# Stick-breaking attention: weights taken as differences of the running product, with value rows differenced instead

## What is computed

```
mask = s_idx < t_idx
log1m = jnp.where(mask, -jax.nn.softplus(z), 0.0)
after = lax.cumsum(log1m, axis=3, reverse=True) - log1m
logw = jax.nn.log_sigmoid(z) + after
w = jnp.where(mask, jnp.exp(...logw...), 0.0)
out = jnp.einsum('bhqk,bhkd->bhqd', w, vb)
```

## Time and profile before

| | |
|---|---|
| median of 3 runs | 2482.05 us (2480.07 to 2483.8) |
| the profiled execution | 2482.8 us, of which the trace spans 2480.7 us |
| PE busy | 2379.0 us, 96% of the span |
| DVE, ACT, POOL busy | 1497.8, 962.1, 672.5 us |
| the values (from the evict of block 0) | 1375 to 1418 us of the span |
| the attention stage | 1418 to 1695 us of the span |

### The profile page before, as it was taken

How to read it: one execution, slowest core, us unless ns; L and a number is a source line. 1 busy time by engine, 2 the same in 40 slices (tenths; PEclk the granted TensorE clock), 3 DMA queues, 4 the chain that set the end, 5 groups by cost and what they waited for, 6 DMA issues and landing times.

```text
span 2480.7 us, 31285 instructions
## 1 busy us (share of the span) xinstructions
PE 2379.0 (96%) x11999; PEld 1919.7 (77%) x11999; DVE 1497.8 (60%) x2510; ACT 962.1 (39%) x1834; POOL 672.5 (27%) x382
## 2 busy tenths in 40 slices
PE   8999978889999999999999999999899999999998
PEld 6678866778888777778888777767688888888886
DVE  3588998662776777864226478773674555553225
ACT  3467837772232323232212255563533323231212
POOL 3013210000234555542223221110223445441220
PEclk9999988999999999999999999999999999999999
DMA  5026451204314554545232210001421322243333
GB/s 178 9 64 190 155 178 56 98 23 157 127 55 134 155 162 145 170 167 187 102 119 77 71 52 28 27 26 69 143 78 56 96 86 69 85 144 111 102 111 119
DMA packets 219980, 259.21 MB, mean 104 GB/s; under 512 B 16540, under 2 KB 150188, under 8 KB 219832
## 3 DMA queue, kind: packets, MB, share of 16 engines
q1 hardware_dynamic: 219832, 257.22, 31.5%
HBM read 197.36 MB, written 59.82 MB: 104 GB/s over the span
## 4 chain that ended last, share of the span: by engine, by line
PE 82%; DVE 10%; DMA 3%; ACT 3%; issue 1%; POOL 1%; SPq 0%; POOLq 0%; DVEq 0%; ACTq 0%
PE bank L546 10%; PE bank L548 10%; PE bank L547 10%; PE bank L1878 8%; PE bank L1879 8%; PE bank L1880 8%; PE bank L520 6%; PE bank L522 6%; PE bank L521 6%; PE bank L1387 2%; DVE res L1322 1%; PE bank L2507 1%; PE bank L2476 1%; DMA early<-in_w_cond 1%; PE bank L2492 1%
## 5 line engine op out<-in xcount | busy, mean ns | idle before, releaser
L498 POOL TENSOR_TENSOR wl<-raw,wh 128x1024 fp32r<-128x1024 f32 x117 | 299.2, 2575 | 1332.9 <-ACT wh L481 1312.9
L546 PE MATMUL bank<-wh,yh 128*128 128x512 f32 x704 | 277.1, 394 | 2.7 <-POOL wl L498 2.6
L547 PE MATMUL bank<-wl,yh 128*128 128x512 f32 x704 | 274.7, 390 | 0.0
L548 PE MATMUL bank<-wh,yl 128*128 128x512 f32 x704 | 274.6, 390 | 0.0
L481 ACT ACTIVATE wh<-raw 128x1024 fp32r<-128x1024 f32 x117 | 123.1, 1060 | 306.3 <-PE bank L548 289.1
L493 POOL TENSOR_TENSOR wl<-res,wh 128x512 fp32r<-128x512 f32 x144 | 198.0, 1397 | 149.2 <-ACT wh L478 125.4
L1878 PE MATMUL bank<-yh,wh 128*128 128x512 f32 x576 | 225.2, 391 | 0.0
L1880 PE MATMUL bank<-yh,wl 128*128 128x512 f32 x576 | 224.1, 389 | 0.0
L1879 PE MATMUL bank<-yl,wh 128*128 128x512 f32 x576 | 224.1, 389 | 0.0
L493 POOL TENSOR_TENSOR wl<-raw,wh 128x512 fp32r<-128x512 f32 x108 | 157.5, 1473 | 228.2 <-ACT wh L478 228.1
L520 PE MATMUL bank<-yh,wh 128*128 128x512 f32 x448 | 182.5, 407 | 8.3 <-DVE yl L583 8.3
(11 more groups left out here) (345 smaller groups left out, 5387.1 us busy)
## 6 DMA issues: line engine op xcount, KB each, us to landing
early<-in_w_cond SPq DMA_DIRECT2D x96, 256.0 KB, 2.9
raw<-in_w_gu SPq DMA_DIRECT2D x44, 512.0 KB, 4.1
raw<-in_w_down SPq DMA_DIRECT2D x44, 512.0 KB, 3.6
raw<-in_w_in SPq DMA_DIRECT2D x40, 512.0 KB, 4.0
qk_d<-res SPq DMA_DIRECT2D x36, 512.0 KB, 4.1
raw<-in_w_gate SPq DMA_DIRECT2D x22, 512.0 KB, 4.1
raw<-in_w_up SPq DMA_DIRECT2D x22, 512.0 KB, 4.2
res<-in_x SPq DMA_DIRECT2D x16, 512.0 KB, 9.9
```

What stands on the lines that cost most here:

```text
L498: pool.i.tensor_tensor(wl[n % NU][:, :], raw_of(u)[:, :], wh[n % NU][:, :].bitcast(F32), ALU.subtract).then_inc(*po.up(("wl", u)))
L546: pe.i.matmul(bank[:, 0:wide], xa, h[:, c:c + wide], start=k == 0, stop=False)
L547: pe.i.matmul(bank[:, 0:wide], xa, l[:, c:c + wide], start=False, stop=False)
L548: last = pe.i.matmul(bank[:, 0:wide], xb_, h[:, c:c + wide], start=False, stop=k == nk - 1)
```

## The change

- A value block is evicted into a new buffer `plain` instead of `vt`. SP then copies it within the on-chip memory into `vt`, one row further down, in three transfers a block (rows 0 to 126; row 127 into row 0 of the next block; row 127 into row tb of `ends`), and DVE subtracts `plain` from `vt` in place. `vt` holds for each key the previous key's value minus its own. Row 0 of the first block takes zeros.
- ACT and DVE split `ends` (8 rows: the last key's values of each block) into `ends_h` and `ends_l`; POOL writes `pick`, eight rows of which row b is 1 in the columns of block b.
- ACT takes one sigmoid a piece (of -z); DVE runs the scan alone; PE transposes the product itself.
- At the start of each of the eight tiles PE adds the last keys' values: two products of 8 rows by 512 columns into the whole bank.
- SP waits for block 7 of the normalised input (`mod2`), then issues the copies of blocks 0 to 5 ahead of the pooling loads, those of 6 and 7 behind them, and `sp_feed` last. DVE subtracts blocks 0, 1, 2 each just ahead of the low parts of turned blocks 5, 6, 7; blocks 3 to 5 behind them; 6 and 7 among the first queries and keys.
- `plain` shares its memory with the first queries and keys, whose evictions wait for the copies.

The core of the diff:

```diff
         def sp_vu():
+            sp.wait_ge(*po.after(("mod2", 7)))
+            for tb in range(6):
+                sp_shift(tb)
             sp.wait_ge(*mm.after(("h", 7, 1)))
-            sp.wait_ge(*po.after(("mod2", 7)))
             sp.i.dma_start(ps4[0:4, :], ...
...
+            for tb in (6, 7):
+                sp_shift(tb)
             sp_feed(v2_units[3])
+        def sp_shift(tb):
+            sp.wait_ge(*av.after(("vu", 0, tb)))
+            c = slice(512 * tb, 512 * tb + 512)
+            sp.i.dma_start(vt[1:128, c], plain[tb][0:127, :]).then_inc(*shifted_in[tb].up(("rows", tb), 16))
+            if tb < 7:
+                after = slice(512 * tb + 512, 512 * tb + 1024)
+                sp.i.dma_start(vt[0:1, after], plain[tb][127:128, :]).then_inc(...)
+            sp.i.dma_start(ends[tb:tb + 1, :], plain[tb][127:128, :]).then_inc(...)
+        def dve_shift(tb):
+            c = slice(512 * tb, 512 * tb + 512)
+            dve.wait_ge(*shifted_in[tb].after(("rows", tb)))
...
+            dve.i.tensor_tensor(vt[:, c], vt[:, c], plain[tb], ALU.subtract).then_inc(*dv.up(("step", tb)))
+        def act_ends():
+            for i in range(2):
+                act.wait_ge(*ends_in[i].after(("end", 4 * i + 3)))
+            act.i.activation(ends_h[0:8, :], ends[0:8, :], ACT.Copy).then_inc(*av.up("ends"))
         def dve_vu():
+            dve_no_token()
             dve_norm2(8)
             for tb in (5, 6, 7):
+                dve_shift(tb - 5)
                 dve_turn("h", tb, yh, yl)
+            for tb in range(3, 6):
+                dve_shift(tb)
         def pe_stick_turn(t):
-            pe.wait_ge(*dv.after(("share", t)))
+            pe.wait_ge(*dv.after(("product", t)))
             for b in range(0, n, 128):
-                last = pe.i.transpose(bank[:, b:b + 128], took[t % 5][:, b:b + 128], idn)
+                last = pe.i.transpose(bank[:, b:b + 128], rest_of[t % 5][:, b:b + 128], idn)
         def pe_stick_weigh(t):
                 pe.wait_ge(*O["r"].prior(("sticko", h, i // 4)))
+                pe.wait_ge(*dv.after("ends"))
+                pe.wait_ge(*po.after("pick"))
+                for e in (ends_h, ends_l):
+                    pe.i.matmul(uses.held["sticko", h, i // 4][:, :], e[0:8, 128 * h:128 * h + 128],
+                                pick[0:8, 512 * (i // 4):512 * (i // 4) + 512], start=e is ends_h, stop=False)
+                pe.wait_ge(*dv.after(("step", 7)))
         act_stick:
-                if t >= 4:
-                    act.wait_ge(*dv.after(("share", t - 4)))
-                    act.wait_ge(*dv.after(("product", t - 2)))
-                act.i.activation(rest_of[t % 4][:, 0:n], z[:, 0:n], ACT.Sigmoid, scale=-1.0).then_inc(*av.up(("rest", t)))
                 if t >= 5:
+                    act.wait_ge(*dv.after(("product", t - 3)))
                     act.wait_ge(*mm.after(("stickt", t - 5)))
-                act.i.activation(took[t % 5][:, 0:n], z[:, 0:n], ACT.Sigmoid).then_inc(*av.frees(uses, ("z", t)))
+                act.i.activation(rest_of[t % 5][:, 0:n], z[:, 0:n], ACT.Sigmoid, scale=-1.0).then_inc(*av.frees(uses, ("z", t)))
         dve_stick:
-                if first:
-                    dve.i.memset(r[:, n:n + 1], 1.0).then_inc(*dv.up())
-                else:
+                if not first:
                     dve.wait_ge(*dv.after(("product", t - 2)))
-                    dve.i.tensor_copy(r[:, n:n + 1], before[:, 0:1]).then_inc(*dv.up())
                 dve.i.tensor_tensor_scan(down, down, down, 1.0 if first else before[:, 0:1], ALU.mult, ALU.bypass ...
-                s_ = took[t % 5]
-                dve.wait_ge(*dv.after(("product", t)))
-                dve.i.tensor_tensor(s_[:, 0:n], s_[:, 0:n], r[:, 1:n + 1], ALU.mult).then_inc(*dv.up(("share", t)))
         dve_sticks:
+                    if a == ("qk2", 0, 1, 1):
+                        dve_shift(6)
+                    if a == ("qk2", 0, 0, 1):
+                        dve_shift(7)
+                        dve_ends()
```

More of the change, by code:

```diff
@@ L211, in build @@
         row_in = [sem(f"row_in{i}") for i in range(2)]
+        shifted_in = [sem(f"shifted_in{i}") for i in range(8)]
+        ends_in = [sem(f"ends_in{i}") for i in range(2)]
         xb_in = [sem(f"xb_in{i}") for i in range(4)]
@@ L289, in build @@
         shared = place[0]
+        plain = [at(f"plain{i}", upper + 4096 + 512 * o, 512)[:, :] for i, o in enumerate((5, 7, 1, 3, 4, 6, 0, 2))]
         ut = [res[:, 1024 * (4 + g):1024 * (4 + g) + 1024] for g in range(4)]
@@ L293, in build @@
         eye16, mask16 = sb("eye16", 128, BF, 64), sb("mask16", 128, BF, 64)
-        rest_of = [sb(f"rest{i}", 513, F32, 520) for i in range(4)]
-        took = [sb(f"took{i}", 512) for i in range(5)]
+        rest_of = [sb(f"rest{i}", 512) for i in range(5)]
         wts = [sb(f"wt{i}", 512) for i in range(2)] + [res[:, 3072:3584], res[:, 3584:4096]]
+        ends_h, ends_l, pick = sb("ends_h", 512, FR), sb("ends_l", 512, FR), sb("pick", 1024, FR)
+        ends = wts[0]
         wp, ps, shares = [sb(f"wp{i}", 128) for i in range(2)], sb("ps", 8), sb("shares", 16)
@@ L2229, in sp_vu, with dve_no_token, pool_pick, dve_ends @@
                 sp_pool_weights(g)
+            for tb in (6, 7):
+                sp_shift(tb)
             sp_feed(v2_units[3])
+        def sp_shift(tb):
[4 more added lines that the diff above has]
+                after = slice(512 * tb + 512, 512 * tb + 1024)
+                sp.i.dma_start(vt[0:1, after], plain[tb][127:128, :]).then_inc(*shifted_in[tb + 1].up(("first", tb + 1), 16))
+            sp.i.dma_start(ends[tb:tb + 1, :], plain[tb][127:128, :]).then_inc(*ends_in[tb // 4].up(("end", tb), 16))
+        def dve_shift(tb):
+            c = slice(512 * tb, 512 * tb + 512)
+            dve.wait_ge(*shifted_in[tb].after(("rows", tb)))
+            if tb == 0:
+                dve.wait_ge(*dv.after("no_token"))
+            dve.i.tensor_tensor(vt[:, c], vt[:, c], plain[tb], ALU.subtract).then_inc(*dv.up(("step", tb)))
+        def dve_no_token():
+            dve.i.memset(vt[0:1, 0:512], 0.0).then_inc(*dv.up("no_token"))
+        def pool_pick():
+            pool.wait_ge(*po.after(("mod2", 7)))
+            pool.i.tensor_copy(pick[0:8, :].rearrange("p (b q) -> p b q", b=8), idn[0:8, 0:8].unsqueeze(2).broadcast_to([8, 8, 128])
+                               ).then_inc(*po.up("pick"))
+        def act_ends():
+            for i in range(2):
+                act.wait_ge(*ends_in[i].after(("end", 4 * i + 3)))
+            act.i.activation(ends_h[0:8, :], ends[0:8, :], ACT.Copy).then_inc(*av.up("ends"))
+        def dve_ends():
+            dve.wait_ge(*av.after("ends"))
+            dve.i.tensor_tensor(ends_l[0:8, :], ends[0:8, :], ends_h[0:8, :].bitcast(F32), ALU.subtract).then_inc(*dv.up("ends"))
         def sp_pool_weights(g):
@@ L2252, in act_vu_out @@
             act.wait_ge(*mm.after(("vu", n, tb)))
-            act.i.activation(vt[:, 512 * tb:512 * tb + 512], uses.held["vu", n, tb][:, :], ACT.Copy
-                             ).then_inc(*av.frees(uses, ("vu", n, tb)))
+            act.i.activation(plain[tb], uses.held["vu", n, tb][:, :], ACT.Copy).then_inc(*av.frees(uses, ("vu", n, tb)))
         def act_vu():
@@ L2437, in act_queries @@
                 act.wait_ge(*after_queries(h - 1, half))
+            else:
+                tb = 4 * (1 - half) + 2 * (1 - n)
+                act.wait_ge(*ends_in[tb // 4].after(("end", tb + 3 - tb % 4)))
+                act.wait_ge(*dv.after(("step", tb + 1)))
             act.i.activation((qs, ks)[n][0][:, 512 * half:512 * half + 512], uses.held[key][:, :], ACT.Copy,
@@ L2447, in dve_queries @@
                 dve.wait_ge(*after_queries(h - 1, half))
+            else:
+                dve.wait_ge(*ends_in[1 - half].after(("end", 7 - 4 * half)))
             dve.i.scalar_tensor_tensor(out=low[:, hs], in0=uses.held[key][:, :], scalar=1.0 if n else 0.125,
@@ L2507, in pe_stick_weigh @@
                     last = pe.i.matmul(ob[r:r + 64, 128 * (i % 4):128 * (i % 4) + 128], vt[:, c:c + 64],
-                                       wts[u % 4][:, 128 * b - c0:128 * b - c0 + 128], start=128 * b == 512 * (i // 4),
-                                       stop=c0 == 0 and 128 * (b + 1) == n)
+                                       wts[u % 4][:, 128 * b - c0:128 * b - c0 + 128], start=False,
+                                       stop=i % 4 == 0 and c0 == 0 and 128 * (b + 1) == n)
             last.then_inc(*mm.up(("weighed", t)))
@@ L2532, in act_stick @@
                     act.wait_ge(*mm.after(("weighed", u - 4)))
+                if u == 0:
+                    act.wait_ge(*dv.after("ends"))
                 act.i.activation(wts[u % 4][:, 0:n], uses.held["stickt", u][:, 0:n], ACT.Copy
@@ L2538, in dve_stick @@
                 h, hh, i, c0, n = pieces[t]
-                r, before = rest_of[t % 4], rest_of[(t - 2) % 4]
+                r, before = rest_of[t % 5], rest_of[(t - 2) % 5]
```

(9 more changed lines are left out.)

5 lines of the change are left out of this document (3 added, 2 removed).

## The result

The changed kernel takes 2535.91 us (median of 4 runs, 2534.08 to 2540.01) against 2482.93 us of the kernel before on the same chip: 1.0215 times the time before, 95% interval 1.02 to 1.0229. The forecast of no change is wrong by 53 us. The profiled execution took 2535.92 us, with a span of 2533.8 us.

The account below looks back on a forecast made before the run. PE was taken to bound the attention stage except its end, where DVE does. Added products +5.3, end of the stage -6.4 and values +2.0 gave +0.9 us, so 2483.0 us: no change (2477.1 to 2487.0), range 2476 to 2489.

Parts of the forecast that it names:

- The values: Ahead of value block 5: DVE waits for block 0's copy, landing at 1400.3, and stalls PE; +2.0 us, at most 4.8.
- over 4 was named as a sign of being wrong: Ahead of value block 5: a PE pause of 2 us was expected; one over 4 us would show the prediction wrong.
- Costed at nothing: SP's last raw load about 4 us later, last values' split, subtractions and `pick` fill: all taken to cost no time.
- copies landing late: Rival, at DVE's wait for block 0: 6.8 us to landing, a 4.8 us stall, 2485.8 to 2487.2 us; chance 0.16.
- What DVE's wait would have cost with a good copy: Ahead of value block 5: PE held up by DVE's wait for block 0's rows, +2.0 us.
- The added products: Start of each tile on PE: sixteen products, 0.66 us a tile, eight tiles, +5.3 us; bounds 3.5 to 6.3.
- The end of the stage: From 1659.1 to 1695.3 us: DVE stays the bound, its freed work gains 6.4 us, about 2.1 us wait left.
- The middle costs nothing: From 1440 to 1659.1 us: PE never idle, so work taken from DVE or ACT gains nothing.
- the rival of short hidden pauses: Full stretch: PE's modelled busy time may hide pauses; if 5 us go, about 2478 us; chance 0.10.
- the fall of the clock that I kept: End of the stage: the clock still falls after PE's remaining pause, no gain; without the fall, 1.4 us lower.
- the 4 to 5 named as a sign: Full stretch: growth by other than 4 to 5 us (seven of eight tiles) would show the prediction wrong.
- No wait left in the end: Rival, end of the stage: the tile's bank is free when PE comes, 10.1 us go, 2479.3 us; chance 0.27.

Follow-up runs that it names:

- experiment 1: The changed kernel with each copy of 127 rows cut into one of 112 and one of 15 rows: 2494.5 us, 1.0016 times the kernel before.
- experiments 4 and 5: experiment 4, and two kernels from the changed one: without its copies (0.9989 times the kernel before), and the scan alone.
- the scan alone: The changed kernel without copies, subtractions, split of last keys' values and sixteen added products; single sigmoid and turned product stay: 0.9954 times the kernel before.
- experiment 4: The changed kernel with copies cut into 112 and 15 rows, blocks 0 to 2 subtracted behind turned blocks' low parts: 2486.92 us, 0.9988 times before; repeated, 0.9995.
- experiment 6: experiment 4 with one added product of 40 rows a tile instead of two of 8 rows: 1.0 times the kernel before.
- the first version of experiment 7: experiment 4 without added products; DVE adds the last keys' values when it copies each full tile out: 2483.79 us, 0.9985 times before.
- experiments 1 and 2: experiment 1, and the changed kernel with its 127-row copy going to the same rows, not one down: 2540.29 us.

## Why the prediction was wrong, point by point

**The step that failed** is in "The values": "The trace has no copy of this kind. Bounds: 2.1 us to landing ... 6.8", and "the other copies are issued behind each other, some 0.4 us each". I bounded the copy by loads of 128 rows, by their bytes. The copy of 127 rows takes 10.6 us of one DMA engine, outside both bounds; DVE gets block 0's rows at 1409.46 instead of 1400.3, PE waits 11.35 us where the term says 2.0 (over 4 was named as a sign of being wrong), and the small copy behind each holds SP's queue for up to 9.6 us instead of 0.4. Even with well cut copies a transfer takes 0.52 to 0.95 us to issue, in most cases, and not 0.4. Two further sentences rested on these: that blocks 1 and 2 "land before DVE comes to them" (8.73 us of wait for block 1), and, in "Costed at nothing", that only SP's last raw load stands behind the copies. The pooling loads that `sp_vu` issues behind block 5 stand there too, and PE waited 23.7 us for them. I had followed each copy to its reader on DVE and not the queue to everything behind it. The rival that named the place, copies landing late, took the same bounds and so gave 2485.8 to 2487.2 where 2535.9 came. Its size was wrong by more than a factor of ten.

The Trainium skill has the rule that spoke against this change (DMA: Bandwidth & Descriptors, "Why a DMA increments its semaphore by 16 and not by 1"): a transfer runs on the largest number of engines up to 16 that divides the slowest dimension of both sides, and it names 127 partitions as a case of one engine. This case's trace agrees: 24.5 GB/s and a share of 0.07 with 127 rows, 82 GB/s and 0.28 with 112 and 15, 81 GB/s and 0.27 with 126 and 1 (from 1405 to 1415 us). The prediction used the same page's fixed cost and not this rule.

**What DVE's wait would have cost with a good copy** (+2.0 us): right for the wait, half of the whole. With copies cut (experiment 1) the first wait of PE is 2.39 us. The step came to 4.3, since another 1.2 us of waits follow and the clock is 0.83 for 10 us, which the sum had at nothing.

**The added products** (+5.3 us, 0.66 a tile): right. The starts of the tile shown are 0.34 and 0.32 apart, 0.66 together; the six tiles of the full stretch cost 214.86 - 211.03 = 3.8 us, 0.64 each, and the first 0.66 (21.31 - 20.65 us, experiments 4 and 5). The upper bound, 16 x 0.39, is 6.2 and not 6.3.

**The end of the stage** (-6.4 us): right. From 32.55 to 24.53 us with the scan alone, -8.0 us. The remaining wait is 1.51 us (forecast 2.1), and the fall of the clock that I kept did not come in that execution, nor in the changed kernel's: with the 1.4 us that I gave for that, the forecast is -7.8. Where it came (experiment 4, clock 0.86) the end took 26.48 us with 0.66 of added products in it, -6.7 without them.

**The middle costs nothing**: right, and the rival of short hidden pauses is ruled out: 211.08, 211.03 and 211.05 us with DVE busy 176 us or 51 us less. With the added products it grew by 3.7 us, a little less than the 4 to 5 named as a sign, since six tiles begin in it and not seven. **No wait left in the end**: false, 1.5 us are left in every version.

**The sum without the failed step**, -6.4 + 5.3 = -1.1 us: experiment 4 has it without the wait, and its stage from the last store to the last weighing is 307.57 us against 308.77, -1.2 us. That it fits to the tenth is in part luck: the clock fell in the end of that execution, and where it didn't (experiment 1) the same end took 1.5 us less.

**Open**: the stretch behind the stage is 785.7 to 785.8 us in the kernel before and with the scan alone, and 786.1 to 788.9 in all others. In nine of them PE waits 0.6 to 1.6 us for DVE once in the feed-forward part (L1847), in experiment 6 and the first version of experiment 7 it does not. Why DVE is late there stays open. The time from the start to the last store differs by up to 10.5 us between executions (1384.94 to 1395.46) though the work there is the same, so the ratios carry this scatter and the stretches don't.

## What to carry to other kernels

Before a transfer is priced by its bytes, look at its number of rows: 126 or 112 rows were shared out among DMA engines, 127 and 31 were not, and cutting 127 into 112 and 15 won 49 us. When a queue gets a new transfer, list everything behind it on that queue with its reader, however small. And where one engine is busy throughout a stretch, work taken off the others is worth only what it gives in the stretches where that engine waits.

## What was not expected of the hardware

**A small copy holds the issuing queue.** A copy of one row (2 KB) took 7.8 to 9.6 us to issue on SP behind the copies of 127 rows (4.72 behind the first), while the next big copy issued in 0.63. Behind well cut copies it took 0.52 to 0.79. Counted in the trace's DMA packets, 98 to 103 rows of the big copies were still to be moved each of the eight times that SP came free. That fits theory A, a queue that waits for room on the busy engine; that a limit of this size is the cause is inferred.

**The same pause with and without a fall of the clock.** The last 12 us up to the last weighing, in the scan alone and in experiment 4 (two kernels; the same columns as above):

```profile
1679.63:1691.63 12.00, 10.03 (x96) 7.62 (x94) 9.78 (x12) 8.26 (x19) 0.00 (x0) 1.00 0.00 0
```

```profile
1686.78:1698.78 12.00, 10.47 (x87) 7.93 (x83) 7.82 (x10) 6.29 (x14) 0.00 (x0) 0.86 0.00 0
```

In both PE waits 0.7, 0.4 and 1.5 us at the same places (the first lies ahead of these 12 us). The granted clock over them is 1.00 in the changed kernel, experiments 1 and 2 and the scan alone; 0.86 in experiment 4 and its repetition, without copies, with 96 and 31 rows and with one product; and 0.72 with 126 and 1 rows. The end of the stage takes 24.5 to 25.0, 26.3 to 26.5 and 28.1 us with it. What decides it these runs don't show.

**The turn between kinds of products.** Between products of full float32 and of float32r, one float32r product costs 0.43 us and each further one 0.20 to 0.23.
